# A router that finds the chosen experts by an eight-largest search, and weight splits moved into the softmax turns of the attention loop

## The reference

```python
pg = jax.nn.softmax((t @ w_rg).astype(jnp.float32), axis=-1)
gp, gi = lax.top_k(pg, 1)
le = (t @ w_re).astype(jnp.float32).reshape(-1, N_GROUPS, EXPERTS_PER_GROUP)
le = jnp.take_along_axis(le, gi[:, :, None], axis=1)[:, 0]
ew, ei = lax.top_k(jax.nn.softmax(le, axis=-1), TOP_K_INNER)
ew = ew / jnp.sum(ew, axis=-1, keepdims=True)
weights = gp * ew
...
logits = jnp.where(valid[:, :, None, :], logits, NEG_BIG)
probs = jax.nn.softmax(logits, axis=-1).astype(v.dtype)
return jnp.einsum('bqhk,bqkd->bqhd', probs, v_sel)
...
merged = jax.nn.sigmoid(ga) * (y_a @ w_branch_a[i]) + jax.nn.sigmoid(gb) * (y_r @ w_branch_b[i])
```

## Time and profile before

| | |
|---|---|
| median of three runs | 1140.06 us (1136.32, 1140.06, 1140.66) |
| the profiled execution | 1140.28 us, its span 1138.5 us |
| busy share of the span | PE 95%, PEld 82%, DVE 62%, ACT 45% |
| mean granted TensorE clock | 0.983 |
| chain that ended last | PE 63%, DVE 13%, ACT 6%, issue 3% |

### The profile page before, as it was taken

The page is one execution under the profiler, slowest core; times in us unless marked ns, Lnnn a source line. Parts: engine busy times, 40 slices in busy tenths (PEclk is TensorE's granted clock), DMA queues, the critical chain, the costliest instruction groups (busy, mean ns, idle before and its releaser), DMA issues.

```text
span 1138.5 us, 19008 instructions
## 1 busy us (share of the span) xinstructions
PE 1086.7 (95%) x7922; PEld 932.7 (82%) x7922; DVE 702.0 (62%) x1141; ACT 513.7 (45%) x803; POOL 0.2 (0%) x4
## 2 busy tenths in 40 slices
PE   5989999899999999899999989898899999999997
PEld 3779888645555554899999979898899999999996
DVE  1889767423323333786865689987656775655667
ACT  3774233211111112754543468477954554443455
POOL 0000000000000000000000000000000000000000
PEclk9999999799999999999999999999999999999998
DMA  9955617999999957557355423433346545545321
GB/s 381 393 198 209 246 71 301 393 419 421 411 405 411 417 225 295 187 181 258 121 213 211 154 91 130 156 141 113 111 160 228 215 162 209 185 167 204 130 94 38
DMA packets 38153, 257.71 MB, mean 226 GB/s; under 512 B 4368, under 2 KB 5264, under 8 KB 7856
## 3 DMA queue, kind: packets, MB, share of 16 engines
q1 hardware_dynamic: 36720, 252.38, 58.1%
q10 hardware_dynamic: 1344, 4.08, 0.9%
HBM read 255.39 MB, written 1.05 MB: 225 GB/s over the span
## 4 chain that ended last, share of the span: by engine, by line
PE 63%; DVE 13%; ACT 6%; issue 3%; DVEq 0%; ACTq 0%
PE bank L540 63%; DVE wl L1820 4%; ACT wh L1251 2%; DVE xt L1870 1%; DVE rstd L1844 1%; ACT arena L1261 1%; ACT L1261 1%; DVE acc L1882 1%; DVE hl L1887 1%; PE bank L927 0%; ACT yl L1261 0%; ACT arena L1652 0%; DVE arena L2401 0%; ACT arena L1599 0%; DVE tn L1902 0%
## 5 line engine op out<-in xcount | busy, mean ns | idle before, releaser
L540 PE MATMUL bank<-hh,wh 128*128 128x256 f32 (+2 forms) x1256 | 363.5, 289 | 5.9 <-issue 1.7
L540 PE MATMUL bank<-hl,wh 128*128 128x256 f32 (+2 forms) x1256 | 359.0, 286 | 0.0
L540 PE MATMUL bank<-hh,wl 128*128 128x256 f32 (+2 forms) x1256 | 358.9, 286 | 0.0
L1820 DVE TENSOR_TENSOR wl<-raw,wh 128x1024 fp32r<-128x1024 f32 (+4 forms) x238 | 267.6, 1164 | 81.3 <-ACT wh L1251 79.3
L1251 ACT ACTIVATE wh<-raw 128x1024 fp32r<-128x1024 f32 (+4 forms) x238 | 227.8, 1003 | 70.0 <-PE bank L540 69.9
L540 PEld LDWEIGHTS bank<-hh,wh 128*128 128x128 f32 (+1 forms) x1256 | 241.4, 192 | 13.7 <-issue 7.8
L540 PEld LDWEIGHTS bank<-hl,wh 128*128 128x128 f32 (+1 forms) x1256 | 241.6, 192 | 1.1
L540 PEld LDWEIGHTS bank<-hh,wl 128*128 128x128 f32 (+1 forms) x1256 | 241.4, 192 | 0.9
L540 PE MATMUL bank<-yh,wh 128*128 128x256 f32 x512 | 146.8, 287 | 0.5 <-DVE yl L1840 0.5
L540 PE MATMUL bank<-yh,wl 128*128 128x256 f32 x512 | 145.5, 284 | 0.0
L540 PE MATMUL bank<-yl,wh 128*128 128x256 f32 x512 | 145.5, 284 | 0.0
(11 more groups left out here) (280 smaller groups left out, 1383.6 us busy)
## 6 DMA issues: line engine op xcount, KB each, us to landing
raw<-in_gu SPq DMA_DIRECT2D x40, 1024.0 KB, 11.2
arena<-in_gu SPq DMA_DIRECT2D x24, 1024.0 KB, 9.8
raw<-in_gd SPq DMA_DIRECT2D x22, 1024.0 KB, 8.4
raw<-in_w_adt SPq DMA_DIRECT2D x14, 1024.0 KB, 5.3
raw<-in_f1g SPq DMA_DIRECT2D x11, 1024.0 KB, 4.7
raw<-in_f1d SPq DMA_DIRECT2D x11, 1024.0 KB, 4.8
raw<-in_f2g SPq DMA_DIRECT2D x11, 1024.0 KB, 4.8
raw<-in_f2u SPq DMA_DIRECT2D x11, 1024.0 KB, 4.8
```

The costliest lines, as they stand in the source:

```text
L540: return pe.matmul(o, l, m, start=start, stop=stop, skip_group_check=True)
L1820: v.tensor_tensor(WL[slot_of[U]][:, 0:n], src, WH[slot_of[U]][:, 0:n].bitcast(f32), ALU.subtract).then_inc(S("wl"), 1)
```

## The change

There are two parts, both in the order or the choice of DVE's instructions. PE, SP and POOL keep every instruction and its order; on ACT one instruction of the router grows from 2 to 64 columns.

The router masks the expert logits of the groups that were not chosen with -3e38 and searches all 32 columns with the instruction that returns the eight largest. The two largest are then marked by replacing every logit equal to one of the first two places: the largest is copied to `chosen`, places 2 to 7 are overwritten with 3e38, and the replacement writes 3e38 where the logits equal places 0 or 1. What is then above 1e38 is `OHE`. The exponentials are taken of all 64 logits minus the largest, and the gate weights follow by a masked sum.

```diff
             first_max(L4, mg, 4, keyg, ohg, kmg)
+            chain(v.tensor_scalar(keyg, ohg, -1.0, 3e38, ALU.add, ALU.mult))
+            chain(v.tensor_tensor(sel, L32, keyg.unsqueeze(3).broadcast_to([128, 2, 4, 8]), ALU.add))
             for a in range(2):
-                step(v.tensor_tensor(sel[:, a], L32[:, a], ohg[:, a, :].unsqueeze(2).broadcast_to([128, 4, 8]), ALU.mult))
+                step(v.max(TOP[:, a, :], EX[:, a, :]))
             prev()
+            step(v.tensor_copy(chosen.unsqueeze(2), TOP[:, :, 0:1]))
+            chain(v.memset(TOP[:, :, 2:8], 3e38))
             for a in range(2):
-                step(v.tensor_reduce(le[:, a, :].unsqueeze(2), sel[:, a].rearrange("p g j -> p j g"), AX.X, ALU.add))
+                step(v.match_replace(REST[:, a, :], TOP[:, a, :], EX[:, a, :], 3e38))
             prev()
-            maxed(m1, le)
-            first_max(le, m1, 8, key1, oh1, km1)
-            chain(v.scalar_tensor_tensor(le2, oh1, -3e38, le, ALU.mult, ALU.add))
-            maxed(m2, le2)
-            first_max(le2, m2, 8, key2, oh2, km2)
-            v.tensor_tensor(ex, m2, m1, ALU.subtract).then_inc(S("ex"), 1)
-            chain(v.tensor_tensor(key1, oh1, oh2, ALU.add))
-            for a in range(2):
-                v.tensor_tensor(OHE4[:, a], ohg[:, a, :].unsqueeze(2).broadcast_to([128, 4, 8]),
-                                key1[:, a, :].unsqueeze(1).broadcast_to([128, 4, 8]), ALU.mult).then_inc(S("ohe"), 1)
+            v.tensor_scalar(OHE3, REST, 1e38, None, ALU.is_gt).then_inc(S("ohe"), 1)
+            v.tensor_tensor(EX, EX, chosen.unsqueeze(2).broadcast_to([128, 2, 32]), ALU.subtract).then_inc(S("ex"), 1)
...
             v.wait_ge(*nth("exx", 1))
-            chain(v.tensor_scalar(sd, ex, 1.0, None, ALU.add))
...
+            chain(v.tensor_tensor(EX, EX, OHE3, ALU.mult))
+            chain(v.tensor_reduce(se.unsqueeze(2), EX, AX.X, ALU.add))
+            chain(v.tensor_tensor(wt.unsqueeze(2), se.unsqueeze(2), sg, ALU.mult))
+            chain(v.reciprocal(wt, wt))
+            v.tensor_tensor(G32E, EX, wt.unsqueeze(2).broadcast_to([128, 2, 32]), ALU.mult).then_inc(S("g32"), 1)
...
-            for h in range(4):
-                ahead("w2rg", h)
-                attention(h)
-                if h == 0:
+            def gated_low(h):
+                v.wait_ge(*nth("rg_h", h + 1))
+                low(YL[:, 2 * h:2 * h + 2, :], YN[:, 2 * h:2 * h + 2, :], YH[:, 2 * h:2 * h + 2, :], "rg_l")
+
+            for n in range(8):
+                c = ("w2rg", n) if n < 4 else ("w2ga", n - 4)
+                attention(n)
+                if 1 <= n < 5:
+                    gated_low(n - 1)
+                split_to(2 * where[c] + AHEAD)
+                if n == 0:
                     ret_var(3)
-                attention_scaled(h)
-                Y2 = YN[:, 2 * h:2 * h + 2, :]
-                evicted(v, ("rg", h))
-                v.wait_ge(*nth("yn", h + 1))
-                v.tensor_tensor(Y2, Y2, TR[h % 2], ALU.mult).then_inc(S("sgy"), 1)
-                v.wait_ge(*nth("rg_h", h + 1))
-                low(YL[:, 2 * h:2 * h + 2, :], Y2, YH[:, 2 * h:2 * h + 2, :], "rg_l")
-            for j in range(4):
-                ahead("w2ga", j)
-                attention(4 + j)
-                attention_scaled(4 + j)
+                attention_scaled(n)
+                split_to(2 * where[c] + 1 + AHEAD)
+                if n < 4:
+                    Y2 = YN[:, 2 * n:2 * n + 2, :]
+                    evicted(v, ("rg", n))
+                    v.wait_ge(*nth("yn", n + 1))
+                    v.tensor_tensor(Y2, Y2, TR[n % 2], ALU.mult).then_inc(S("sgy"), 1)
```

More of the change, by code:

```diff
@@ L189, in program @@
         TRI, IOTA, LG = ar(0, 128), ar(128, 128), ar(256, 72).rearrange("p (a e) -> p a e", a=2)
-        mg, e4, sg, gp = ar(328, 2).unsqueeze(2), pair(ar(330, 8)), ar(338, 2).unsqueeze(2), ar(340, 2).unsqueeze(2)
+        mg, e4, sg = ar(328, 2).unsqueeze(2), pair(ar(330, 8)), ar(338, 2).unsqueeze(2)
         L4, L32 = LG[:, :, 0:4], LG[:, :, 4:36].rearrange("p a (g j) -> p a g j", g=4)
@@ L195, in program @@
         sel = ar(378, 64).rearrange("p (a g j) -> p a g j", a=2, g=4)
[L196 to L200, removed]
+        TOP, REST, EX = pair(ar(442, 16)), pair(ar(458, 64)), pair(ar(378, 64))
+        chosen, se, wt = (ar(546 + 2 * i, 2) for i in range(3))
         G32 = ar(554, 64).rearrange("p (a g j) -> p a g j", a=2, g=4)
@@ L835, in tensor_program @@
             pe.wait_ge(*nth("d_t", 32))
-            pe.wait_ge(*nth("ohe", 2))
+            pe.wait_ge(*nth("ohe", 1))
             mm(b[:, 0:32], TRI, OHE3[:, 0, :], True, True)
@@ L1442, in scalar_program @@
             a.wait_ge(*nth("ex", 1))
-            a.activation(ex, ex, ACT.Exp).then_inc(S("exx"), 1)
+            a.activation(EX, EX, ACT.Exp).then_inc(S("exx"), 1)
             def summed_highs(first):
@@ L2144, in vector_program @@
             v.wait_ge(*nth("rank", 1))
-            v.wait_ge(*nth("ohe", 2))
+            v.wait_ge(*nth("ohe", 1))
             step(v.tensor_reduce(MX, bank("rank")[:, 64:96], AX.X, ALU.max))
@@ L2164, in vector_program @@
             chain(v.tensor_reduce(sg, e4, AX.X, ALU.add))
-            chain(v.reciprocal(gp, sg))
             v.wait_ge(*nth("exx", 1))
-            chain(v.tensor_scalar(sd, ex, 1.0, None, ALU.add))
[L2168 to L2178, removed]
+            chain(v.tensor_tensor(EX, EX, OHE3, ALU.mult))
[3 more added lines that the diff above has]
+            v.tensor_tensor(G32E, EX, wt.unsqueeze(2).broadcast_to([128, 2, 32]), ALU.mult).then_inc(S("g32"), 1)
+            v.wait_ge(*nth("g32", 1))
             G32P = ar(554, 64).rearrange("p (a j e) -> p a j e", a=2, j=16)
```

## The result

The changed kernel takes 1132.62 us (median of nine runs, 1131.96 to 1134.91) against 1137.89 for the kernel before beside it (nine runs, 1135.74 to 1140.66): 5.3 us less, a ratio of 0.995 with an interval of 0.9937 to 0.9963. The direction was forecast. The fall from 1140.28 that the forecast gave was 3.4; the profiled execution of the changed kernel took 1134.31 (span 1132.5), 6.0 less than that of before. Two kernels of the experiments also had much slower runs (1143.02 for the one with both edits, 2121.44 and 2693.94 for the one with the wait filled), which are left out of their medians.

What follows compares the result with a forecast made beforehand. PE, busy 95% of the span, was taken to bound the kernel. From 1140.28 us, 1.6 for the router and 1.8 for the attention loop were subtracted, giving 1136.9, with a range of 1133.2 to 1139.8.

Steps and rivals of the forecast that it cites:

- PE bounds; shifts pass through the experts: Whole kernel: PE, busy 95% of the span, sets the pace, so an earlier router end passes through the experts.
- The search's price: Router: DVE's new chain from key to OHE sums to 1.84 us, small forms priced by a straight line from wider ones.
- The whole wait of 1.61 goes: gain 1.6: Router: OHE is ready before PE's transposes end, so PE's idle time goes; gain 1.6 us, bounds 1.3 and 1.8.
- Rival B: Router: without PE's break the clock rises earlier, up to 3.6 us more won, 1135.1 to 1133.3; chance 0.20.
- A: Whole kernel: the forecast itself, router and loop gains together, 1136.9 us (1135.9 to 1138.0); chance 0.57.
- The loop, 1.8: Attention loop: turns 1 and 2 win 1.1 each, turn 3 wins 0.3, turn 0 loses 0.7; together 1.8 us.
- The second split's cost of 0.04: Attention loop: DVE's second split, now ahead of the gated product, delays it by only 0.04 us, leaving the 0.76 wait.
- C: Attention loop: the reorder wins nothing, through the second split's delay or the table load's hidden time; 1138.7 us, chance 0.10.
- D: Router: the change doesn't shorten the wait, or the experts absorb it; 1138.5 us, chance 0.04.
- E: Attention loop: the second split is late for PE, 1 us in each of eight turns; slower, 1146.7 us, chance 0.03.
- F: Attention loop: the clock falls more often, perhaps two falls more; 1139.4 us, or 1141.2 without the loop's gain; chance 0.06.
- nothing is corrected: Base: the profiled execution's 1140.28 us, 0.2 above the median of 1140.06, was used unadjusted.

Runs made afterwards that it cites:

- both edits: Changed kernel with DVE's splits behind the gated product in turns 0 and 3 and ACT's first split ahead of the high part: 1126.55 us.
- the wait filled: Kernel before, with three matmuls of 256 columns that compute nothing ahead of PE's wait for OHE: 0.999 of the kernel before.

## Why the prediction was wrong, point by point

Of the 4.3 by which the forecast missed the time, 2.4 is the base (1140.28 against a median of 1137.89) and 1.9 the fall (3.4 against 5.3). In the fall the router's term was too small, above all for the clock behind the wait, which had been left out of the sum, and the loop's term was too small by less.

**PE bounds; shifts pass through the experts: right.** The router's 2.7 still stand at 467 us, 2.5 are there at 728 and 3.0 at 736.

**The search's price: nearly right.** Counted from the same link, the chain takes 1.67 where the sum has 1.84: copy and memset took 0.23 for 0.33, the replacements with their loads 0.45 for 0.52. The small forms cost what the straight line said, to 0.02. The new gate part has six instructions for eleven, not for twelve; nothing hung on that.

**"The whole wait of 1.61 goes: gain 1.6": this step failed.** It held DVE's old chain against PE's transposes as they ran in one execution. The chain is fixed (4.37 behind the exponential in four traces with the old search, 2.5 with the new), but PE's side is not: where the transposes ran at 2.4 GHz the wait was 3.29 and 3.30. The gain at the rank matmuls is therefore 1.8 to 1.9, not capped at 1.6 by PE. That is the upper bound given, 1.8, and the smaller part of what the router's term missed.

**Rival B is what happened beside A, and it should have been in the sum.** The second interval is 8.0 to 8.6 with the old search and 6.5 where the clock comes back early (7.8 in the profiled execution, where the rise at 208.3 still was 3.7 earlier). That PE's idle time has a part in it, the thirteen traces show: a wait of 0.97 put back gives 8.88 in one, and the old wait filled with matmuls gives 6.49 in another. The times of these two kernels do not confirm it. Taken over the traces, the router's section is 12.4 to 13.0 before and 9.0 to 9.1 in seven of the eight traces with the new search and no delay (10.38 in the eighth): it is worth 3.3 to 4.0, rather than 1.6, and 2.6 in the profiled pair. By the times the router alone gave 3.0 (1.8 to 5.0).

I gave B 0.20 because the stretch before the break was at 1.2 GHz too. That argument failed: in all nine traces with the new search the transposes ran at 1.2 GHz for most of their time (3.4 to 3.7 us), and in seven the clock was back with the rank matmuls. Had they run at 2.4 GHz, PE would still wait some 1.4 (3.3 less 1.9, an estimate from the old search's traces); no trace shows what the clock does then.

The Trainium skill (TensorE: Matmul & The Clock Gate, section What's actually happening) says that the gate's monitor runs free of the program; two executions of the changed kernel agree, with the clock back at 208.3 in one and at 202.9 in the other.

**The loop, 1.8: the mechanism was right, two terms were mis-sized.** Turns 1 and 2 won 1.11 and 1.10, as the sum has it (1.1 each). Turn 0 lost 0.32 instead of 0.7: its exponentials came 1.0 earlier, for DVE waited only 0.50 for the scores, and the high part's wait grew by 1.34 (2.27 for 0.93). Turn 3 won 0.58 instead of 0.3. I had let L2447's wait hold the exponentials; the trace has DVE's `attention` at 789.51, the moment that ACT's copy is out, while ACT itself needs until 791.16 for the next copy and its table load, so 1.05 were won; 0.47 went back in the longer wait ahead of the high part (1.22 for 0.76). Together 2.47, and 2.47 again with the old router. The upper bound of 2.6 in the working was itself too low: its own bounds, 1.1 in each of turns 1 to 3 and no loss in turn 0, add up to 3.3.

**The second split's cost of 0.04: right in turns 1 and 2** (wait 0.76 as before), wrong in turns 0 and 3, where DVE has no idle time for it.

**C, D, E, F.** The loop alone won 2.6 and the router alone 3.0, each clear of zero by its interval, so C and D are out; against C also stands that the table load at 773.86 is followed by its exponentials after 1.29. E didn't occur in the changed kernel, though splits placed behind the product in turn 3 brought just that wait, 2.2 us. One fall of the clock stands in the loop of the profiled execution, as before, so F didn't occur either.

**The base.** The step "nothing is corrected" failed too. The sum was made against 1140.28, near the median of the three runs shown; the next six runs brought that to 1137.89. From there the same sum gives 1134.5, and the whole range, moved along, would have held the measured time. With the terms right (router 2.6 to 4.0, loop 2.5) the fall is 5.1 to 6.5, which holds the measured 5.3 and 6.0.

## What to carry to other kernels

A wait of one engine seen in one profile is the difference of two chains; price its removal from the chain that you shorten, and look at how much faster the waiting engine could have come to that place. Where the waiting engine is PE, an idle time can cost its length and the clock behind it: a wait of 1.61 by its row was worth 2.6 to 4.0 in the traces. Filling it with matmuls that compute nothing gave 1.5 to 2.1 of that in one trace, and in the times nothing that can be told from noise. A split that an engine has time for in some turns of a loop stands in the way in the first and last of them; ordering those turns by themselves gave nothing clear alone. Let the engine that waits (here ACT, ahead of the high part) do the next turn's work there, which gave 3.4 us more. And a base taken from one execution carries that execution's clock: look at several runs before the terms are subtracted.

## What the runs showed of the hardware

In one execution with an idle time of 0.97 us of PE the granted clock stayed at 0.50 for more than 7 us behind it, PE being busy; in one without it, from the same level at the same place, the clock came back after 5.5. In two executions of the old router the clock fell inside an idle time of 3.3. The place where the clock is down moves from execution to execution of one program (in the kernel before the transposes ran at either level), and runs of one program differ by up to 5.7 us (1136.36 to 1142.09). The two go together: of the 17 runs of the kernel before in the last group the five shortest (1136.48 to 1136.80) had a mean granted clock of 0.985 to 0.989 and the four longest (1140.53 to 1142.16) one of 0.981 to 0.984. That the place in the router causes the difference was not shown run by run.
